# Middle layer norm and per-layer embedding of a decoder trunk in one block on Trainium2

## What is computed

```
mix = concat(y_ssd, y_gla, y_mla) @ w_out
x   = layernorm(ALPHA * x + mix) * ln1_g + ln1_b                  # the middle norm
ple = sigmoid(x @ ple_w_gate) * (p[layer] @ ple_w_proj)           # the per-layer embedding
f   = ConvGLU(x)                                                  # ffn_w_up, conv, gelu, ffn_w_down
x   = layernorm(ALPHA * x + f + ple)
```

## Time and profile before

| | us |
|---|---|
| median of 3 runs (lowest, highest) | 2362.07 (2361.13, 2362.76) |
| the profiled execution | 2367.72 |
| its span in the trace | 2365.9 |
| PE busy | 2060.7 (87%) |
| DVE, ACT, POOL busy | 944.5, 774.1, 654.4 |

### The profile page before, as it was taken

How to read it: one execution, slowest core, us unless ns; L and a number is a source line. 1 busy time by engine, 2 the same in 40 slices (tenths; PEclk the granted TensorE clock), 3 DMA queues, 4 the chain that set the end, 5 groups by cost and what they waited for, 6 DMA issues and landing times. The chain is left out here.

```text
span 2365.9 us, 39388 instructions
## 1 busy us (share of the span) xinstructions
PE 2060.7 (87%) x16323; PEld 1874.0 (79%) x16323; DVE 944.5 (40%) x1477; ACT 774.1 (33%) x1395; POOL 654.4 (28%) x332
## 2 busy tenths in 40 slices
PE   4998896789879999989959988947979899999996
PEld 3997663668869999989859965636868799999995
DVE  3332534744332333345416045365442143333553
ACT  4333323143241222233344232323332422222433
POOL 0441100610222444334224311034113234333440
PEclk8998875589789999999979977756989999999998
DMA  2431003054112222222033210020812032323210
GB/s 93 133 63 38 7 5 102 1 206 166 40 46 90 72 92 86 81 84 97 10 105 90 28 44 1 23 84 18 296 63 72 28 108 72 107 71 107 67 63 38
DMA packets 168755, 177.25 MB, mean 75 GB/s; under 512 B 47198, under 2 KB 151302, under 8 KB 166340
## 3 DMA queue, kind: packets, MB, share of 16 engines
q1 hardware_dynamic: 163884, 132.58, 18.3%
q0 software_dynamic: 4608, 41.95, 4.8%
q10 hardware_dynamic: 100, 0.46, 0.1%
HBM read 166.11 MB, written 8.86 MB: 74 GB/s over the span
## 5 line engine op out<-in xcount | busy, mean ns | idle before, releaser
L337 POOL TENSOR_TENSOR w_low<-ring,w_high 128x1024 fp32r<-128x1024 f32 x120 | 290.9, 2425 | 615.7 <-ACT w_high L333 615.7
L356 PE MATMUL ps<-x_high,w_high 128*128 128x272 f32 x1664 | 347.3, 291 | 28.3 <-DVE x_low L347 22.3
L333 ACT ACTIVATE w_high<-ring 128x1024 fp32r<-128x1024 f32 x166 | 174.8, 1055 | 541.8 <-PE ps L356 487.8
L356 PE MATMUL ps<-x_low,w_high 128*128 128x272 f32 x1664 | 344.2, 288 | 0.0
L356 PE MATMUL ps<-x_high,w_low 128*128 128x272 f32 x1664 | 343.3, 288 | 0.0
L356 PEld LDWEIGHTS ps<-x_high,w_high 128*128 128x128 f32 x1664 | 261.8, 189 | 30.0 <-DVE x_low L347 23.2
L356 PEld LDWEIGHTS ps<-x_low,w_high 128*128 128x128 f32 x1664 | 263.3, 190 | 0.0
L356 PEld LDWEIGHTS ps<-x_high,w_low 128*128 128x128 f32 x1664 | 262.5, 189 | 0.0
L356 PE MATMUL ps<-x_high_in,w_high 128*128 128x272 f32 x736 | 154.3, 291 | 44.9 <-POOL w_low_in L337 44.9
L2538 DVE TENSOR_SCALAR arena<-arena,parb 128x560 f32<-128x560 f32 x44 | 84.4, 1918 | 273.0 <-ACT arena L2486 273.0
L337 POOL TENSOR_TENSOR w_low_in<-ring,w_high 128x1024 fp32r<-128x1024 f32 x46 | 109.8, 2389 | 270.8 <-ACT w_high L333 270.8
(11 more groups left out here) (400 smaller groups left out, 3527.9 us busy)
## 6 DMA issues: line engine op xcount, KB each, us to landing
ring<-in_ffn_w_up SPq DMA_DIRECT2D x44, 1024.0 KB, 5.8
ring<-in_ffn_w_down SPq DMA_DIRECT2D x20, 1024.0 KB, 5.1
ring<-in_w_in SPq DMA_DIRECT2D x18, 1024.0 KB, 5.4
ring<-in_w_out SPq DMA_DIRECT2D x8, 1024.0 KB, 7.1
ring<-in_ple_w_gate SPq DMA_DIRECT2D x8, 1024.0 KB, 5.1
big<-in_state_ssm SPq DMA_DIRECT2D x16, 256.0 KB, 4.4
out_ssm_sample<-big SPq DMA_DIRECT2D x4, 1024.0 KB
arena<-in_x_prompt SPq DMA_DIRECT2D x1, 2048.0 KB
```

Of the source, the lines that this page charges most:

```text
L333: act.activation(wh[:, i % 2], ring[:, n % RING, :, c0:c0 + P], ACT.Copy).then_inc(s_high, 1)
L337: pool.tensor_tensor(low[:, i % 2], ring[:, n % RING, :, c0:c0 + P], wh[:, i % 2].bitcast(F32), ALU.subtract).then_inc(s_low, 1)
L356: last = pe.matmul(ps[:, b + h, 0:HALF], w[:, i % 2, k, :], x[:, k, h * HALF:(h + 1) * HALF], start=(k == 0 and x is x_high and w is wh), ...
```

## The change

The norm loses its call of `layer_norm`, and its work and that of the embedding become one block:

- The embedding rows and `ple_w_proj` are loaded at the end of the block of the output projection, on SP's queue behind the fourth gate load, into the space of `mixT`, whose halves have been made by then. `ple_w_proj` needs no slot of the ring any more; `ffn_w_up` begins at load 20, and a slot of the gate weights is given free after two products.
- PE's order is: mean, transpositions of the rows and of the convolution parameters, sum of the squares, eight embedding products, eight gate products. The embedding products go through two pairs of banks; of the first six, DVE copies the even and ACT the odd ones to SBUF (`pP`), and the last two stay in PSUM.
- ACT: high halves of two gate weights, squares, copy of the convolution parameters, logarithm, exponential; then per tile the bias, a wait for it, the high half, and after tiles 1, 4 and 7 a kept product. DVE: centring, copies of the transposed rows, then scalings, low halves and kept products interleaved.
- POOL makes all eight low halves of the gate weights and the first two of the up-projection, and waits for its own last one before the block ends.

The diff, cut:

```diff
-        N_IN, LD_OUT, LD_GATE, LD_PROJ, LD_UP, LD_DOWN = 12, 12, 16, 20, 21, 43
+        N_IN, LD_OUT, LD_GATE, LD_UP, LD_DOWN = 12, 12, 16, 20, 42
-        PR_UP = PR_PLE + 2 * KD
+        PR_UP = PR_PLE + KD
...
-            if n < LD_PROJ:
-                return PR_PLE + 2 * 2 * (n - LD_GATE + 1)
+            if n < LD_UP:
+                return PR_PLE + 2 * (n - LD_GATE + 1)
...
                                                   w_cols(a["ple_w_gate"], L, 0, KD, c0, c0 + 256))])
+
+                    e.wait_ge(s_ml, KD)
+                    e.dma_start(ptok[:, 0:PT, :], a["p_prompt"][L, 0].rearrange("(j p) c -> p j c", p=P)
+                                ).then_inc(s_ple, 16)
+                    e.dma_start(ptok[0:NS, PT, :], a["p_sample"][L].rearrange("b l c -> (b l) c")).then_inc(s_ple, 16)
+                    e.dma_start(pw, a["ple_w_proj"][L].rearrange("(k p) n -> p k n", p=P)).then_inc(s_ple, 16)
...
-            layer_norm("ln1", lambda k: col(k, G1), lambda k: col(k, B1), summed=True,
-                       ahead=(split_gate_high, split_gate_low))
...
                 @block.gpsimd
                 def _(e):
-                    for m in range(2, KD):
-                        e.wait_ge(s_wh, m - 1)
+                    for m in range(KD):
+                        e.wait_ge(s_wh, m + 1)
                         low_weights(m, LD_GATE + m // 2, (m % 2) * P, wl, s_wl)
                     for part in range(2):
-                        e.wait_ge(s_wh, KD - 1 + part)
+                        e.wait_ge(s_wh, KD + 1 + part)
                         low_weights(part, LD_UP + part, 0, wl, s_wl)
+                    e.wait_ge(s_wl, KD + 2)
...
                 @block.tensor
                 def _(e):
                     def transposed_rows():
 
-                        e.wait_ge(s_pin, 32)
+                        e.wait_ge(s_ple, 48)
...
+                    def layer_products(m):
+                        if m == 0:
+                            e.wait_ge(s_ptk2, 4)
                         if m >= 2:
+                            e.wait_ge(s_pk2 if m % 2 == 0 else s_pk3, m // 2)
                         for k in range(2):
                             for h in range(2):
+                                last = pe.matmul(ps[:, p_banks(m) + h, 0:HALF], pw[:, k, m * P:(m + 1) * P],
                                                  pT[:, k, h * HALF:(h + 1) * HALF], start=(k == 0), stop=(k == 1))
+                        last.then_inc(s_pp, 1)
+
+                    for h in range(2):
+                        last = pe.matmul(ps[:, h, 0:HALF], C("mean"), xsum[:, h * HALF:(h + 1) * HALF],
+                                         start=True, stop=True)
+                    last.then_inc(s_mean, 1)
+                    transposed_rows()
+                    for k in range(KD):
+                        e.wait_ge(s_sq, k + 1)
+                        for h in range(2):
+                            last = pe.matmul(ps[:, 2 + h, 0:HALF], C("mean"), sq[:, k, h * HALF:(h + 1) * HALF],
+                                             start=(k == 0), stop=(k == KD - 1))
+                    last.then_inc(s_var, 1)
+                    for m in range(KD):
+                        layer_products(m)
+                    for m in range(KD):
+                        e.wait_ge(s_wl, m + 1)
+                        if m >= 2:
+                            e.wait_ge(s_sg, m - 1)
+                        split_product(e, m, 2 * (m % 2), wl, xh, xl, s_xl if m == 0 else None)
...
                 @block.scalar
                 def _(e):
...
+                    for k in range(KD):
+                        e.wait_ge(s_nrm, k + 1)
+                        act.activation(xT[:, k], xT[:, k], ACT.Identity, bias=col(k, B1)).then_inc(s_bia, 1)
+                        e.wait_ge(s_bia, k + 1)
+                        act.activation(xh[:, k], xT[:, k], ACT.Copy).then_inc(s_xh, 1)
+                        if k in (1, 4, 7):
+                            product_kept(1 + 2 * (k // 3))
...
                 @block.vector
                 def _(e):
...
+                    scaled(0)
+                    scaled(1)
+                    product_kept(0)
+                    for k in range(KD):
+                        if k + 2 < KD:
+                            scaled(k + 2)
+                        low(k)
+                        if k in (2, 5):
+                            product_kept(2 * (k // 3) + 2)
...
+                        if m < 6:
+                            e.wait_ge(s_pk2 if m % 2 == 0 else s_pk3, m // 2 + 1)
+                            dve.tensor_tensor(mixT[:, m], mixT[:, m], pP[:, m], ALU.mult).then_inc(s_pm, 1)
```

More of the change, by code:

```diff
@@ L2372, in high, with product_kept @@
                         high_weights(m, LD_GATE + m // 2, (m % 2) * P, s_wh)
-                    high_x(xh, xT, s_xh)
+                    def product_kept(m):
+                        e.wait_ge(s_pp, m + 1)
+                        act.activation(two(pP[:, m]), halves(p_banks(m)), ACT.Copy).then_inc(s_pk3, 1)
+                    high(0)
+                    high(1)
+                    for k in range(KD):
+                        e.wait_ge(s_ctr, k + 1)
+                        act.activation(sq[:, k], xT[:, k], ACT.Square).then_inc(s_sq, 1)
+                    e.wait_ge(s_ptr2, 2)
+                    act.activation(parb[:, :, :], ps[:, 7, 0:20 * KF].rearrange("p (k r) -> p k r", r=20),
+                                   ACT.Copy).then_inc(s_ptk2, 1)
+                    e.wait_ge(s_var, 1)
+                    act.activation(two(lv), halves(2), ACT.Ln, bias=C("eps_ln"))
+                    e.drain()
+                    act.activation(rstd, lv, ACT.Exp, scale=-0.5).then_inc(s_rstd, 1)
+                    for k in range(KD):
[5 more added lines that the diff above has]
+                            product_kept(1 + 2 * (k // 3))
                     for m in range(KD):
@@ L2377, in _ @@
                             high(m + 2)
[L2378 to L2387 removed]
+                        act.activation(two(mixT[:, m]), halves(2 * (m % 2)), ACT.Sigmoid).then_inc(s_sg, 1)
                     for part in range(2):
@@ L2390, in _, with product_kept, scaled @@
                         high_weights(part, LD_UP + part, 0, s_wh)
-                    e.wait_ge(s_wh, KD)
+                    e.wait_ge(s_wh, KD + 2)
                 @block.vector
                 def _(e):
-                    low_x(e, xl, xT, xh, s_xh, s_xl)
+                    def product_kept(m):
+                        e.wait_ge(s_pp, m + 1)
+                        dve.tensor_copy(two(pP[:, m]), halves(p_banks(m))).then_inc(s_pk2, 1)
+                    def scaled(k):
+                        dve.scalar_tensor_tensor(out=xT[:, k], in0=xT[:, k], scalar=col(k, G1), in1=rstd,
+                                                 op0=ALU.mult, op1=ALU.mult).then_inc(s_nrm, 1)
@@ new lines, in low @@
+                    def low(k):
+                        e.wait_ge(s_xh, k + 1)
+                        dve.tensor_tensor(xl[:, k], xT[:, k], xh[:, k].bitcast(F32), ALU.subtract).then_inc(s_xl, 1)
+                    e.wait_ge(s_mean, 1)
+                    for k in range(KD):
+                        dve.tensor_tensor(two(xT[:, k]), two(xT[:, k]), halves(0), ALU.subtract).then_inc(s_ctr, 1)
+                    e.wait_ge(s_ptr2, 1)
+                    for k in range(2):
+                        dve.tensor_copy(pT[:, k, 0:SEQ], ps[:, 4 + k, :]).then_inc(s_ptk2, 1)
```

74 lines of the change are left out of this document (27 added, 47 removed).

## The result

The changed kernel took 2367.95 us (median of 20 runs) beside 2362.13 us for the kernel before: a ratio of 1.0023, interval 1.0014 to 1.0032. In a second comparison it was 1.0014, interval 0.9996 to 1.0032 (2367.05 beside 2361.35 us), which just includes no change. So it is slower by some 3 to 5 us; I had predicted no change, with a range that holds the result.

What follows compares the result with a forecast made beforehand. PE, busy 87% of the span, was taken to bound the kernel. First layer -0.8 and second +0.7 us summed to 0 within the working: 2362.0 us predicted, range 2352 to 2375.

Steps and rivals of the forecast that it cites:

- the mean of the squares: PE in the norm, behind the transpositions: 7.4 us at the full clock (above 9.66), ending 7.0 us late.
- the rival with late rows: Loads before the norm land after about 675, squares' mean starts in the low clock: +3.6 and +2.2 per layer, 2373.6; chance 0.17.
- the logarithm: Sign in the norm, behind the squares' mean: it comes 7 us later than before.
- Rows: Loads before the transpositions: embedding rows and projection weights landed by 673.0 (bounds 672.5 and 676.6).
- Transpositions: PE, between mean and squares' mean: 5.1 us in the low clock after idling (below 2.65, above 5.3).
- the cheap cover: Rival in the norm: transpositions at full clock (2.65), ScalarE chain packed (13.2): -4.4 per layer, 2353; chance 0.20.
- Scaling to gate: From first scaling to first gate product, embedding products between: 15.2 us (below 13.2, above 17.0).
- Tail: Between last gate product and up-projection: PE idle 7.4 us where it was 3.0 (bounds 7.1 and 7.9).
- The fallen clock: Rival in the embedding products: clock falls in the sparse stretch, six products at 3.7 us: +9.2 per layer, 2380; chance 0.11.
- The first up product: Start of the up-projection, behind 7.4 idle us: 8.06 us, giving back 0.3 in the first layer, 1.8 in the second.
- the first part: Stretch from last output product to logarithm: predicted +7.0 us in each layer.
- the last: Stretch from up-projection to the copy of its first product: predicted +0.3 and +1.8 us in the two layers.

Runs made afterwards that it cites:

- early rows: Changed kernel with the three loads of rows and projection weights issued ahead of the gate loads: 2346.08 us, 0.9923 of the kernel before; second time 2348.57 us, 0.9945.
- half of the weights once more: Changed kernel with half of the projection weights (0.5 MB) loaded a second time, the transpositions waiting for it too: 2368.83 us, 1.0032 of the kernel before.
- the shorter tail: Changed kernel with high halves of the first two up weights made ahead of the seventh and eighth sigmoid: 2366.42 us, 1.0019 of the kernel before.
- the first experiment: Changed kernel with the squares' mean ahead of all transpositions, ACT's parameter copy behind the exponential: 2354.3 us, 0.9966 of the kernel before.
- the run with the small transpositions moved: Changed kernel with only the 22 convolution-parameter transpositions behind the squares' mean, their copy behind the exponential: 2363.97 us, 1.0006 of the kernel before.

## Why the prediction was wrong

The path was as forecast, and so were most steps: PE waits for the rows and holds the squares' mean behind the transpositions, the gate starts later and the embedding products leave its path. One term was mis-sized, because what brings the clock up was taken wrongly, and it carries the sign: with its 7.4 us the sum would have come out 0.6 us per layer below the old kernel instead of 1.7 above.

**The failing step** is the mean of the squares, put at the full clock, 7.4 us. It took 9.62, 9.49, 9.63 and 10.18, by the mean 9.73: 2.3 us per layer more, just beyond the bound of +2.2. At the full clock it does take 7.60 (early rows), so the size of the term was right for the clock that was assumed, and the clock was not. The squares' mean in the low clock was priced in the rival with late rows, and came about though the rows were not late. The reason given was that "the clock rose 4 us after PE had begun to work without a break". PE did work without a break, but on transpositions, and these did not bring the clock up: in the changed kernel it rose 8.7 us after their start, and where 22 of them were moved away, 5.6 us after, both times 3 to 4 us after the squares' mean began; in the kernel before, where nothing stands in front of that mean, it rose about 4 us after it too.

The other passes say the same. With all 32 transpositions in front and the clock low (the changed kernel twice, half of the weights once more, the shorter tail: eight passes) it rose 7.5 to 10.5 us after PE took them up, but 2.9 to 5.9 us after the squares' mean began; with none in front (the kernel before twice, the first experiment: six passes) 2.8 to 6.1 us after. The Trainium skill, "TensorE: Matmul & The Clock Gate", section "Part 4: PE-mode transpose", says that the full clock does not engage for transpositions. These runs agree for the 32 together, with one limit: transpositions that came while the clock was up ran at the full rate (10 in 1.27 us, with the early rows). Whether the ten large ones alone bring the clock up no run separates, nor whether the 22 fail to because they are transpositions or because they are so small. Why the rise after the start of the squares' mean is early in one pass and late in another was not tried.

**The other steps.** Of the signs named beforehand the logarithm failed: it came 9.6 us later and not 7. Rows: I had the transpositions 9.4 us after the last output product (673.0 - 663.6), measured 9.6; the late rows did not come about. Transpositions 5.1, measured 4.6, at the low clock as forecast; so the cheap cover fell too, though the early rows show that it was there to be had. Scaling to gate 15.2, measured 15.07 (708.18 - 693.11); the lower bound of 13.2 does not follow from its own terms, which give 13.5 without handoffs (0.8 + 16 x 0.56 + 1.9 + 1.85). Tail 7.4 us idle, measured 7.19. The fallen clock did not show in this kernel's embedding products (1.00 from 691 to 708), but in the run with the small transpositions moved it did, behind 1.77 us of idle time, in both layers, and cost 1.5 us in each (logarithm to gate 20.45 us instead of the 18.94 of the run with all transpositions behind, where 0.77 us of idle time stood there and the clock stayed at 1.00).

**A smaller miss the other way.** The first up product: I had +1.8 us in the second layer, from the one row of 6.28. Over four passes before it was 7.80, 6.29, 7.82, 7.84, after 7.59, 7.56, 7.62, 7.85. So +2.6 us for the first part (2.3 from the squares' mean, the rest from passes in which the old one was quicker than in the rows I had) and -0.8 for the last make +1.7 per layer where I had 0.

**What the change lost.** It took 14.9 us per layer off the stretch from the first gate product to the up-projection and gave 16.4 back ahead of it (9.6 + 6.8), and 0.2 in the first up product. Some 10.6 of these are one placement: three loads issued behind a gate load that waits for the last output product. Their space is free some 43 us sooner (with the early rows they are issued from 623.69 on, and the last gate load at 667.32), and their place in the queue is all that kept them.

## What to carry to other kernels

When work is moved to fill a hole, look at what it waits for: on an engine that works in order, a filler that is late delays the chain it was to hide behind, and its loads belong ahead of any load that waits for a slot. An idle time can cost twice, itself and the low clock behind it: here 0.97 us ahead of the up-projection left the clock up, 4.6 and 7.2 us never did, and what lies between went either way. Where such an idle time remains ahead of a long product, price that product at both clocks, and do not count on transpositions to bring the clock back: 4.6 us of them did not do it here. A rate that was read from one pass wants a second profiled execution before it carries a term.

## What the runs showed that I had not expected

VectorE's product of sigmoid and kept embedding, both from SBUF, takes 2.50 us where it meets GpSimd's low half (timeline of the changed kernel, first layer):

```profile
721.73 2.40 POOL L338 TENSOR_TENSOR w_low<-ring,w_high 128x1024 fp32r<-128x1024 f32 x1 [3.61 <-ACT w_high L334]
722.20 2.50 DVE L2453 TENSOR_TENSOR mixT<-mixT,big 128x544 f32<-128x544 f32 x1 [2.73 <-ACT mixT L2409]
```

GpSimd's instruction ends at 724.13 and VectorE's 0.57 us later. VectorE's next instruction, also on two tiles in SBUF but with GpSimd idle, took 0.72. The wait lies beside the gate product, and the eight gate products still follow each other every 6.05 us. The Trainium skill, "SBUF — State Buffer", section "Who interferes with whom", says that a VectorE instruction with two SBUF inputs contends with a GpSimd instruction that reads SBUF, and that the port pair they share is an exclusive lock. The row agrees: VectorE's product ends only behind GpSimd's instruction.

And the length of an idle time does not by itself say how slow the next product is. The first up product took 6.3 us behind 0.97 or 1.25 us of idle time (four passes), 6.3 to 7.8 behind 3.0 us (four), 8.8 to 9.1 behind 4.6 us (four), and behind 7.2 us 7.6 to 9.0 (sixteen passes, 13 of them at 8.1 or less). What matters is when the clock comes back: in the changed kernel it rose about 3 us after the product's start, in the passes near 9 us 5.7 to 6.2 us after it. What decides between the two was not tried.
